# The first matrix of expert n+1 ahead of the second matrix of expert n, in a decoder step with 32 experts

## The chip, the cores and the metric

One core of a Trainium2 chip runs the whole program. The metric is the device time of one execution in microseconds, as the median of several runs of the same program. The engines named below are TensorE (PE in the profile, PEld for its weight loads), VectorE (DVE), ScalarE (ACT), GpSimd (POOL) and SyncE (SP). SP does nothing but wait and issue transfers here.

## The reference, cut to what matters

One layer is applied to 256 prompt tokens and 8 sample tokens that share all weights: a mixer (pooling and a matrix memory), a layer norm, 32 experts of which each token uses four, a second layer norm and a gated embedding. Everything is float32. The part that the change touches is the experts:

```
def run_block(args):
    e, toks, g = args
    xb = xf[toks]
    h = xb @ w1[e] + b1[e]                       # 1024 -> 2048
    glu = jnp.minimum(h[:, ::2], SWIGLU_LIMIT)
    lin = jnp.clip(h[:, 1::2], -SWIGLU_LIMIT, SWIGLU_LIMIT)
    a = glu * jax.nn.sigmoid(SWIGLU_ALPHA * glu) * (lin + 1)
    out = a @ w2[e] + b2[e]                      # 1024 -> 1024
    return out * g[:, None].astype(out.dtype)
...
x2 = layer_norm(DN_ALPHA * x1 + ff, ln2_g, ln2_b)
y = x2 + jax.nn.sigmoid(x2 @ w_ple_gate) * (p.astype(x2.dtype) @ w_ple)
```

All 32 experts' weights are read once from HBM: 8 MiB of `w_mlp1` and 4 MiB of `w_mlp2` for each.

## The kernel before

**The weight ring.** `ring` has 16 slots of 1 MiB (8 KiB in each of 128 partitions). An expert takes 12 units of one slot: 8 for its first matrix, 4 for its second. SP loads them two at a time ("a pair", 2 MiB, `load_pair`, line 396). Units are numbered in order of use, and unit v may be loaded when TensorE has used unit v-16: each use of a unit raises the semaphore `units_used`, and SP waits for it before each pair. So 8 pairs at most are loaded or in flight ahead of TensorE. The first 16 units are loaded during the mixer. Two of them lie in the slots 10 and 11 that hold the state `Cst` until it is written out, so unit 6 waits for the semaphore `C_out` of that store. GpSimd issues that store (line 1900), and after it eight small output transfers (lines 1903 to 1912), the gate table (lines 1914 to 1921) and two loads of layer norm columns (line 1926).

**One expert** (`expert(n, j)`, once each on TensorE, VectorE and ScalarE). A body of `STEP = 4` experts stands in a loop on each engine; `passes` of blocks of 64 places are made, one with these inputs. TensorE's order for expert n is written out by hand:

1. biases of the first matrix (line 870), then 8 units of it (line 883), into `bank[0]` and `bank[1]`. After units 1, 3 and 5 come the three parts of `combine` for expert n-1 (lines 844 and 850): the rows that `eout` holds are spread back to tokens. VectorE adds them to the totals (`accumulate`, lines 1395 and 1400).
2. `gather(n + 1)` (line 822) collects the next expert's rows, `spread_places` (line 836) makes the pattern for the next combine.
3. four transposes of the activation `act_out` (line 907), which VectorE and ScalarE have made in the meantime from `bank[0]` and `bank[1]` (lines 1424 to 1430, sigmoid in line 1744). ScalarE copies the result to `aT` (line 1749).
4. `turn_gathered` (line 857) for the next expert, of which VectorE makes `xgT` (lines 1385 and 1388).
5. bias of the second matrix (line 914), then its 4 units (line 925) into `bank[4]`, which ScalarE copies to `eout` (line 1752).

**Before the loop** stand the routing, `gather(0)`, `turn_gathered`, `spread_places(0)` and the last piece of an early embedding. VectorE starts the totals (line 1460) and ScalarE copies parts of the gate table once GpSimd has made it (lines 1761 and 1765, semaphore `sample_moved`).

**After the loop** TensorE transposes a piece of the embedding's input, waits for `eout`, does the last combine into `LAST_BANKS`, an embedding product (line 975), transposes of the normalised rows (line 988) and the gate product (line 1001). Its weights (`w_ple`, and four loads of `w_ple_gate` into slots 6 to 9, line 464) are issued by SP behind the last expert's.

Of the kernel before, what the change touches and what calls it, by code (L numbers as in the profile page):

```python
# [22 lines left out]
P = 128  # L23
# [13 lines left out]
FF = 1024  # L37
# [13 lines left out]
UNITS = 12  # L51
FIRST = 4
# [45 lines left out]
def build(nc, consts, x_prompt, x_sample, state_pool, state_C, state_n, state_m, p_prompt, p_sample,  # L98
# [4 lines left out]
    with ExitStack() as ctx:  # L103
# [162 lines left out]
        sel = sb("sel", [3 * EXPERTS, 2, P], BF16)  # L266
# [48 lines left out]
        def slot_of(body_unit):  # L315
            return (FIRST + body_unit) % SLOTS

        def landings(body_unit):

            s = slot_of(body_unit)  # L320
            return sum(slot_of(v) == s for v in range(body_unit + 1))
# [6 lines left out]
        def _(sp):  # L328
# [65 lines left out]
            def load_pair(e, j, u):  # L394
                s = slot_of(UNITS * j + u)
                sp.dma_start(pair_place(s), pair_weights(e, u)).then_inc(sem(f"slot{s}"), 16)


            def load_next(n):

                load_pair(n // UNITS, n // UNITS, n % UNITS)

# [15 lines left out]
            load_next(10)  # L418
            sp.wait_ge(sem("hT_ps"), 2)
# [9 lines left out]
            for n in range(SLOTS, UNITS * STEP, 2):  # L429
                sp.wait_ge(sem("units_used"), n - SLOTS + 2)  # L430
                load_next(n)

            def load_body(e, done):

                for n in range(0, UNITS * STEP, 2):
                    sp.wait_ge(sem("units_used"), done + (n - SLOTS + 2))
                    load_pair(e + n // UNITS, n // UNITS, n % UNITS)

            bodies = EXPERTS // STEP
            with sp.Fori(1, bodies) as i:  # L440
                load_body(i * STEP, i * (STEP * UNITS))
            sp.wait_ge(sem("passes_ready"), 1)
            npass = sp.value_load(extra[0:1, 0:1], min_val=0, max_val=PASSES - 1) + 1
            with sp.If(npass > 1):
                with sp.Fori(1, npass) as b:
                    with sp.Fori(0, bodies) as i:
                        load_body(i * STEP, b * (EXPERTS * UNITS) + i * (STEP * UNITS))
            sp.nop()


            used = npass * (EXPERTS * UNITS)

            def wait_slot(s):
                sp.wait_ge(sem("units_used"), used + ((s - FIRST) % SLOTS + 1 - SLOTS))
# [6 lines left out]
            for i in range(4):  # L461
                if 6 + i == 8:
                    wait_slot(9)
                sp.dma_start(ring[:, 6 + i, :].rearrange("p (k n) -> p k n", k=2),
                             w_ple_gate[0, 256 * i:256 * i + 256, :].rearrange("(k p) n -> p k n", p=P))\
                  .then_inc(sem(f"pgate_in{i}"), 16)
# [18 lines left out]
        def _(pe):  # L485
# [374 lines left out]
            def expert(n, j):  # L860

                i4 = n - j

                pe.wait_ge(sem("xgT_done"), n + 1)

                pe.wait_ge(sem("h_read"), n * 2 + 1)
                for t in range(2):
                    for q in range(2):
                        col = FF * t + 512 * q
                        pe.matmul(bank[q][BLOCK * t:BLOCK * (t + 1), :], sel[:, j % 2, 0:BLOCK],  # L870
                                  bias_parts[:, col:col + 512], start=True, stop=False)
                for k in range(KD):
                    u = UNITS * j + k
                    s = slot_of(u)

                    if k % 2 == 0:
                        pe.wait_ge(sem(f"slot{s}"), i4 * 12 + 16 * (before[s] + landings(u)))
                    if k == 5:
# [9 lines left out]

                    if k == 1:
                        pe.wait_ge(sem("out_done"), n + 1)  # L890
                        pe.wait_ge(sem("comb_read"), n * 3 + 1)
                        combine(0, (j + 1) % 2)
                    elif k == 3:
                        pe.wait_ge(sem("comb_read"), n * 3 + 2)
                        combine(1, (j + 1) % 2)
                    elif k == 5:
                        combine(2, (j + 1) % 2)

                pe.wait_ge(sem("onehot_ready"), n * 2 + 4)
                gather(n + 1)  # L900
                pe.wait_ge(sem("hotT_done"), n + 1)
                spread_places((j + 1) % 2)

                for m in range(4):
                    if m == 0:
                        pe.wait_ge(sem("act_ready"), n * 2 + 2)
                    last = pe.transpose(bank[3][:, m * P:(m + 1) * P], act_out[:, m * P:(m + 1) * P], ident)  # L907
                last.then_inc(sem("aT_ps"), 1)
                pe.wait_ge(sem("xg_copied"), n + 2)
                turn_gathered()  # L910

                pe.wait_ge(sem("comb_read"), n * 3 + 4)
                for h in range(2):
                    pe.matmul(bank[4][BLOCK * h:BLOCK * (h + 1), :], sel[:, j % 2, 0:BLOCK],  # L914
                              bias_parts[:, 2 * FF + 512 * h:2 * FF + 512 * h + 512], start=True, stop=False)
                pe.wait_ge(sem("aT_done"), n + 1)
                for k in range(8):
                    u = UNITS * j + 8 + k // 2
                    s = slot_of(u)
                    if k % 4 == 0:  # L920
                        pe.wait_ge(sem(f"slot{s}"), i4 * 12 + 16 * (before[s] + landings(u)))
                    w = ring[:, s, :].rearrange("p (a f) -> p a f", a=2)
# [4 lines left out]
                    if k % 2 == 1:  # L927
                        last.then_inc(sem("units_used"), 1)

# [20 lines left out]
            pe.wait_ge(sem("h_read"), npass * (2 * EXPERTS) + 1)  # L950
            pe.wait_ge(sem("xgT_done"), npass * EXPERTS + 1)
# [6 lines left out]
            pe.wait_ge(sem("hotT_done"), npass * EXPERTS + 1)  # L958
            combine(0, (STEP - 1) % 2, LAST_BANKS[0])
            combine(2, (STEP - 1) % 2, LAST_BANKS[2])  # L960
            pe.wait_ge(sem("xg_copied"), npass * EXPERTS + 1)
# [6 lines left out]
            def gate_weights(k):  # L968
                return ring[:, 6 + k // 2, :].rearrange("p (k n) -> p k n", k=2)[:, k % 2, :]
# [61 lines left out]
        def _(dve):  # L1031
# [372 lines left out]
            def expert(n, j):  # L1404

                for c in range(2):
                    dve.wait_ge(sem("comb_ps"), n * 3 + 1 + c)
                    accumulate(c, n, (bank[7], bank[4]))

                dve.wait_ge(sem("gathered"), n + 1)  # L1410
                dve.wait_ge(sem("out_done"), n + 1)
                one_hot(n + 1, (j + 1) % 2)
                dve.wait_ge(sem("comb_ps"), n * 3 + 3)
                if j == 0:
                    dve.wait_ge(sem("sample_moved"), 7)
                accumulate(2, n, (bank[7], bank[4]))

                for q in range(2):
                    if q == 0:
                        dve.wait_ge(sem("first_half"), n + 1)  # L1420
                    else:
                        dve.wait_ge(sem("units_used"), n * UNITS + 8)
# [3 lines left out]
                    dve.wait_ge(sem("halves_ready"), n * 4 + 2 * q + 2)  # L1426
                    STT(lin[:, q, :], lin[:, q, :], 1.0, glu[:, q, :], ALU.add, ALU.mult).then_inc(sem("h_read"), 1)  # L1427
                    dve.wait_ge(sem("h_read"), n * 2 + q + 2)
                    dve.wait_ge(sem("sig_ready"), n * 2 + q + 1)
# [3 lines left out]
                hot_turned(n + 1, (j + 1) % 2)  # L1433
                turned(n + 1)
# [34 lines left out]
            hot_turned(0, 0)  # L1469
            dve.wait_ge(sem("ple_ps"), 3)  # L1470
# [7 lines left out]
            with dve.Fori(0, npass * EXPERTS, STEP) as n:  # L1478
                for j in range(STEP):
                    expert(n + j, j)  # L1480
# [469 lines left out]
```

## Time and profile before

| | us |
|---|---|
| time, median of 3 runs (lowest, highest) | 1123.28 (1123.21, 1123.94) |
| span of the profiled execution, first to last instruction | 1122.0 |
| the profiled execution's own time, by its span | 1122.0, which is 1.3 below the median of the runs |
| TensorE busy | 1102.2 (98% of the span) |
| VectorE, ScalarE, GpSimd busy | 410.8, 165.4, 78.3 |
| HBM read | 436.61 MB |

The span is that of one execution and leaves out what lies before the first and after the last instruction; times of runs are therefore a little above it. TensorE is called busy while a matmul is in its pipeline, so a high share doesn't say by itself that it sets the time. The DMA share in a stretch is the mean over the core's 16 DMA engines. It can come out a little above 1.00, since a packet is counted where it starts.

### The profile page before, as it was taken

How to read it: one execution, taken by the hardware profiler on the slowest of the kernel's cores; microseconds unless marked ns; L12 is line 12 of the kernel's file. 1: busy time of each engine (PE TensorE's matmuls, PEld its weight loads, DVE VectorE, ACT ScalarE, POOL GpSimd, SP SyncE). 2: the span in 40 equal slices, each digit the busy share in tenths (PEclk: the TensorE clock that was granted, in tenths of full speed). 3: DMA queues.
4: the chain of work that ended last, by engine and by line, in shares of the span. 5: the costliest groups of instructions: out<-in, count | busy, mean ns of one | idle time of the engine just before them, and what ended most of it. 6: DMA issues, size and time to landing. Idle time of an engine off the chain costs nothing.

```text
span 1122.0 us, 14800 instructions
## 1 busy us (share of the span) xinstructions
PE 1102.2 (98%) x5706; PEld 428.6 (38%) x5706; DVE 410.8 (37%) x875; ACT 165.4 (15%) x310; POOL 78.3 (7%) x102
## 2 busy tenths in 40 slices
PE   8999999999999999999999999999999999999998
PEld 6788433333333333333333333333333333323344
DVE  1657583333333333333333333333333333222255
ACT  1423141001000100010001100010001000100033
POOL 0756610000000000000000000000000000000000
PEclk9999999999999999999999999999999999999999
DMA  9986779999999999999999999999999999999961
GB/s 318 261 341 240 253 286 403 427 428 428 429 428 429 429 427 429 427 429 428 430 428 428 429 427 429 429 429 428 428 429 428 429 429 429 427 429 427 428 280 39
DMA packets 47699, 440.45 MB, mean 393 GB/s; under 512 B 10512, under 2 KB 11788, under 8 KB 22741
## 3 DMA queue, kind: packets, MB, share of 16 engines
q1 hardware_dynamic: 46489, 436.94, 93.8%
q0 software_dynamic: 896, 2.66, 0.8%
q10 hardware_dynamic: 292, 0.56, 0.1%
q8 instruction: 13, 0.21, 0.1%
q14 instruction: 9, 0.07, 0.0%
HBM read 436.61 MB, written 3.77 MB: 392 GB/s over the span
## 4 chain that ended last, share of the span: by engine, by line
PE 87%; DMA 10%; DVE 2%; ACT 0%; issue 0%; SPq 0%; DVEq 0%; ACTq 0%
PE bank L883 36%; PE bank L925 18%; DMA ring<-in_w_mlp 9%; PE bank L822 7%; PE bank L510 6%; PE bank L844 5%; PE bank L1001 2%; PE bank L686 2%; PE bank L857 2%; PE bank L907 2%; PE bank L870 1%; PE bank L914 1%; PE bank L850 1%; DMA ring<-in_w_in 1%; PE bank L836 1%
## 5 line engine op out<-in xcount | busy, mean ns | idle before, releaser
L883 PE MATMUL bank<-ring,proj 128*64 128x512 f32 x2048 | 466.0, 597 | 4.7 <-DMA ring<-in_w_mlp 4.7
L1395 DVE SCALAR_TENSOR_TENSOR xT<-bank,proj,xT 128x512 f32<-128x512 f32 x128 | 90.2, 747 | 440.9 <-PE bank L844 439.5
L883 PEld LDWEIGHTS bank<-ring,proj 128*64 128x64 f32 x2048 | 135.3, 136 | 288.7 <-issue 246.9
L925 PE MATMUL bank<-ring,wpool 128*64 128x512 f32 x1024 | 225.1, 592 | 0.0
L925 PEld LDWEIGHTS bank<-ring,wpool 128*64 128x64 f32 x1024 | 71.2, 136 | 130.0 <-issue 129.2
L1744 ACT ACTIVATE proj<-proj 128x256 f32<-128x256 f32 x64 | 26.7, 417 | 546.7 <-DVE proj L1424 546.7
L822 PE MATMUL bank<-xreg,proj 128*64 128x512 f32 (+1 forms) x396 | 95.4, 599 | 0.1
L510 PE MATMUL bank<-xT,ring 128*128 128x264 f32 x320 | 76.3, 396 | 2.9 <-DVE proj L1058 2.4
L844 PE MATMUL bank<-mixT 64*128 64x512 f32 x264 | 74.5, 641 | 0.5 <-ACT mixT L1752 0.5
L510 PEld LDWEIGHTS bank<-xT,ring 128*128 128x128 f32 x320 | 61.4, 195 | 15.6 <-DVE proj L1058 2.8
L1752 ACT COPY mixT<-bank 128x512 f32<-128x512 f32 x32 | 18.8, 586 | 232.4 <-PE bank L925 232.4
L1424 DVE TENSOR_SCALAR proj<-bank 128x256 f32<-128x256 f32 x64 | 26.7, 417 | 67.4 <-PE bank L883 67.4
L822 PEld LDWEIGHTS bank<-xreg,proj 128*64 128x64 f32 (+1 forms) x396 | 25.3, 134 | 64.7 <-issue 64.7
L1400 DVE SCALAR_TENSOR_TENSOR hist_mix<-bank,proj,hist_mix 128x128 f32<-128x128 f32 x66 | 20.1, 347 | 70.1 <-PE bank L850 70.1
L1430 DVE TENSOR_TENSOR proj<-proj 128x256 f32<-128x256 f32 x64 | 38.8, 605 | 5.0
L844 PEld LDWEIGHTS bank<-mixT 64*128 64x128 f32 x264 | 19.9, 184 | 52.9 <-issue 52.9
L1385 DVE TENSOR_TENSOR proj<-bank,ln_rows_of_pairs 128x512 f32<-128x512 f32 x33 | 22.8, 692 | 19.2 <-PE bank L857 19.1
L686 PE MATMUL bank<-ring,mixT 128*128 128x512 f32 x64 | 28.7, 597 | 0.1
L1001 PE MATMUL bank<-ring 128*128 128x512 f32 (+1 forms) x80 | 28.2, 509 | 0.2 <-issue 0.2
L1427 DVE SCALAR_TENSOR_TENSOR proj<-proj 128x256 f32<-128x256 f32 x64 | 27.2, 425 | 2.2
L1425 DVE TENSOR_SCALAR proj<-bank 128x256 f32<-128x256 f32 x64 | 26.3, 411 | 0.0
L857 PE MATMUL bank<-cst,hist_mix 128*128 128x128 f32 x132 | 24.6, 309 | 0.2 <-ACT hist_mix L1755 0.2
(339 smaller groups left out, 633.6 us busy)
## 6 DMA issues: line engine op xcount, KB each, us to landing
ring<-in_w_mlp SPq DMA_DIRECT2D x192, 2048.0 KB, 23.8
ring<-in_w_in SPq DMA_DIRECT2D x10, 1024.0 KB, 12.4
ring<-in_w_out SPq DMA_DIRECT2D x4, 1024.0 KB, 8.4
ring<-in_w_ple_gate SPq DMA_DIRECT2D x4, 1024.0 KB, 27.9
xreg<-in_x_prompt SPq DMA_DIRECT2D x4, 512.0 KB, 4.7
ring<-q_row SPq DMA_DIRECT2D x1, 2048.0 KB, 7.1
ring<-k_row SPq DMA_DIRECT2D x1, 2048.0 KB, 7.0
out<-ring POOLq DMA_DIRECT2D x1, 2048.0 KB, 14.2
```

The lines of the kernel that those rows point to most:

```text
L510: last = pe.matmul(bank[t % 2][:, 0:TOK], w[:, k % 4, j * P:(j + 1) * P], xT[:, k, :], start=(k == 0), stop=(k == KD - 1))
L686: last = pe.matmul(banks[half][0:n, :], mixT[:, k, t0:t0 + n], w[:, k % 2, half * 512:half * 512 + 512], start=(k == 0), stop=(k == KD - 1))
L822: last = pe.matmul(bank[2][BLOCK * h:BLOCK * (h + 1), :], onehot[0:m, c, 0:BLOCK], xtok[0:m, c, 512 * h:512 * h + 512], start=(c == 0), st ...
L844: last = pe.matmul(banks[h][:, :], hotT[half, buffer, c * P:(c + 1) * P], eout[half, :], start=True, stop=True)
L857: last = pe.transpose(bank[6][:, q * P:(q + 1) * P], xg_of_pairs[:, q // 2, q % 2, :], ident)
L883: last = pe.matmul(bank[q][BLOCK * t:BLOCK * (t + 1), :], xgT[:, k % 4, k // 4, :], ring[:, s, col:col + 512], start=False, stop=(k == KD ...
L925: last = pe.matmul(bank[4][BLOCK * h:BLOCK * (h + 1), :], aT[:, m, BLOCK * t:BLOCK * (t + 1)], w[:, k % 2, 512 * h:512 * h + 512], start=F ...
L1001: last = pe.matmul(GATE_BANKS[c][i], x2T[:, k, t0:t0 + n], gate_weights(k)[:, PIECES[c][i]], start=(k == 0), stop=(k == KD - 1))
L1395: ins = STT(total[:, c, s], ins_bank[h][:, :], gate_table[:, c, bass.ds(n, 1)], total[:, c, s], ALU.mult, ALU.add)
L1424: TS(glu[:, q, :], hb[:, 0, :], LIMIT, None, ALU.min).then_inc(sem("halves_ready"), 1)
L1427: STT(lin[:, q, :], lin[:, q, :], 1.0, glu[:, q, :], ALU.add, ALU.mult).then_inc(sem("h_read"), 1)
L1430: TT(act_out.rearrange("p (a q x) -> p q x a", a=4, q=2)[:, q], lin[:, q, :].rearrange("p (x a) -> p x a", a=4), sig[:, q, :].rearrange("p ...
```

## The change

TensorE's order becomes, for step n: the first matrix of expert n+1 with the combine of expert n-1 in it, `gather(n + 2)`, `spread_places`, the first half of the second matrix of expert n, `turn_gathered`, its second half, and the transposes of the activation of n+1. VectorE and ScalarE follow the same order. The first matrix of expert 0, its activation and `gather(1)` move ahead of the loop, with no combine in them. The loop covers all but the last four experts, whose steps are written out behind it: the last but one step has nothing to gather any more, and the last has no first matrix and does its combine into other banks (`LATE_BANKS`) before the second matrix.

The order of the loads follows the order of use: 8 units of expert 0's first matrix, then in turn 8 units of the first matrix of n+1 and 4 of the second of n. Behind the first matrix of expert 31 eight units are left out, so that the last second matrix lands in the slots 8 to 11, which that first matrix used; the gate's weights go to the slots 1, 3, 6 and 7. `sel` gets four buffers in place of two. The store of `Cst` moves from GpSimd's queue to SP's, behind the load of unit 10, and GpSimd's descriptor scratch is 2048 bytes in place of 8192.

```diff
+LEAD = 8
-        sel = sb("sel", [3 * EXPERTS, 2, P], BF16)
+        sel = sb("sel", [3 * EXPERTS, STEP, P], BF16)
+        GATE_SLOTS = (1, 3, 6, 7)
+        LATE_BANKS = {0: (bank[7], bank[2]), 1: (bank[0], bank[1]), 2: (bank[5], bank[6])}
...
+            def load_next(v):
+                n, u = divmod(v - LEAD, UNITS)
+                if v < LEAD:
+                    load_pair(0, v, v)
+                else:
+                    load_pair(n + 1 if u < 8 else n, v, u)
...
             sp.wait_ge(sem("Cnew_done"), 1)
             load_next(10)
+            sp.dma_start(C_sample[0].rearrange("b h v k -> v (b h) k"), Cst).then_inc(sem("C_out"), 16)
...
+            def load_body(e, done, following):
+                for r in range(0, UNITS * STEP, 2):
+                    j, u = divmod(r, UNITS)
+                    first = u < 8
+                    if first and j == STEP - 1 and following is None:
+                        continue
+                    sp.wait_ge(sem("units_used"), done + (LEAD + r - SLOTS + 2))
...
+            tail = npass * (EXPERTS * UNITS) - STEP * UNITS
+            load_body(last, tail, None)
...
+            def step(n, j, ahead=2):
+                i4 = n - j
+                v0 = LEAD + UNITS * j
+                if ahead >= 1:
+                    first_matrix(n + 1, j + 1, v0, i4, n)
+                    if ahead == 2:
+                        pe.wait_ge(sem("onehot_ready"), n * 2 + 6)
+                        gather(n + 2)
+                    pe.wait_ge(sem("hotT_done"), n + 1)
+                    spread_places((j + 1) % STEP)
+                    pe.wait_ge(sem("comb_read"), n * 3 + 4)
+                else:
+                    pe.wait_ge(sem("h_read"), n * 2 + 3)
+                    pe.wait_ge(sem("hotT_done"), n + 1)
+                    pe.wait_ge(sem("xg_copied"), n + 1)
+                    pe.wait_ge(sem("out_done"), n + 1)
+                    pe.wait_ge(sem("comb_read"), n * 3 + 1)
+                    for c in range(3):
+                        combine(c, (j + 1) % 2, LATE_BANKS[c])
+                second_matrix(n, j, v0 + 8, i4, range(0, 4))
+                if ahead == 2:
+                    pe.wait_ge(sem("xg_copied"), n + 3)
+                    turn_gathered()
+                second_matrix(n, j, v0 + 8, i4, range(4, 8))
+                if ahead >= 1:
+                    turn_activation(n + 1)
...
+            first_matrix(0, 0, 0, 0)
+            pe.wait_ge(sem("onehot_ready"), 4)
+            gather(1)
+            turn_activation(0)
+            pe.wait_ge(sem("xg_copied"), 2)
+            turn_gathered()
             pe.wait_ge(sem("ln1_in"), 48)
...
-            with pe.Fori(0, npass * EXPERTS, STEP) as n:
+            with pe.Fori(0, npass * EXPERTS - STEP, STEP) as n:
                 for j in range(STEP):
-                    expert(n + j, j)
+                    step(n + j, j)
+            for j in range(STEP):
+                step(npass * EXPERTS - STEP + j, j, min(2, STEP - 1 - j))
...
(VectorE, ahead of the loop)
+            dve.wait_ge(sem("gathered"), 1)
+            one_hot(1, 1)
...
+            dve.wait_ge(sem("sample_moved"), 7)
+            activate(0, LEAD)
+            turned(1)
...
(ScalarE, in a step)
+                act.wait_ge(sem("units_used"), n * UNITS + (LEAD + UNITS if ahead else LEAD + UNITS - 8))
                 act.copy(eout, bank[4][:, :]).then_inc(sem("out_done"), 1)
+                if ahead >= 1:
+                    turned_activation(n + 1)
...
(GpSimd)
             pool.engine_nop().then_inc(sem("Cnew_done"), 1)
-            pool.dma_start(C_sample[0].rearrange("b h v k -> v (b h) k"), Cst).then_inc(sem("C_out"), 16)
...
-    nc = bacc.Bacc("TRN2", target_bir_lowering=False, num_devices=1, dynamic_dma_scratch_size=8192)
+    nc = bacc.Bacc("TRN2", target_bir_lowering=False, num_devices=1, dynamic_dma_scratch_size=2048)
```

## Rows read from the trace of the kernel before

**Rows 1.** The page: packets of the instruction queue; a small load's size and time to landing.
```profile
q8 instruction: 13, 0.21, 0.1%
...
cst<-in_consts ACTq DMA_DIRECT2D x1, 64.0 KB, 3.9
```
**Rows 2.** Windows: stretch, length, each engine's busy time, clock, DMA share, GB/s.
```profile
160.00:164.00 4.00, 3.75 (x19) 1.33 (x20) 3.76 (x13) 0.59 (x1) 1.32 (x2) 1.00 0.03 12
...
192.00:900.00 708.00, 708.00 (x3659) 232.91 (x3657) 227.45 (x475) 71.94 (x130) 0.00 (x0) 1.00 1.01 428
```
**Rows 3.** Chain that ended last, through one expert: start, length, what.
```profile
502.34 0.43 PE bank L870 x4
502.77 3.44 PE bank L883 x16
506.21 1.06 PE bank L844 x4
...
515.50 0.36 PE bank L850 x16
...
519.44 2.72 PE bank L822 x12
...
522.38 0.59 PE bank L907 x4
...
523.93 6.87 PE bank L925 x32
530.80 0.43 PE bank L870 x4
```
**Rows 4.** Pairs of weights on SP's queue, line 396: when issued, time to landing.
```profile
L396 SPq DMA_DIRECT2D ring<-in_w_mlp x1: 328/328/328, 122.4 to 122.4; - x1
DMA to landing us min/median/max: 8.5/8.5/8.5
...
L396 SPq DMA_DIRECT2D ring<-in_w_mlp x1: 328/328/328, 164.8 to 164.8; - x1
DMA to landing us min/median/max: 9.9/9.9/9.9
...
L396 SPq DMA_DIRECT2D ring<-in_w_mlp x1: 328/328/328, 185.9 to 185.9; - x1
DMA to landing us min/median/max: 8.8/8.8/8.8
...
L396 SPq DMA_DIRECT2D ring<-in_w_mlp x1: 333/333/333, 1036.1 to 1036.1; - x1
DMA to landing us min/median/max: 35.3/35.3/35.3
```
**Rows 5.** Chain that ended last, at the first expert.
```profile
160.67 0.63 PE bank L870 x4
```
**Rows 6.** Timeline at the first expert: start, length, engine, line; [idle before, releaser].
```profile
162.59 3.31 POOL L1921 TENSOR_SCALAR proj<-proj 128x160 f32<-128x160 f32 x3 [24.39 <-DVE proj L1325]
...
167.07 1.69 ACT L1765 COPY hist_mix<-proj 8x256 f32<-8x256 f32 x4
...
180.18 0.60 DVE L1430 TENSOR_TENSOR proj<-proj 128x256 f32<-128x256 f32 x1
...
181.37 0.74 PE L857 MATMUL bank<-cst,hist_mix 128*128 128x128 f32 x4
...
182.87 0.69 DVE L1388 TENSOR_TENSOR proj<-proj,ln_rows_of_pairs 128x512 f32<-128x512 f32 x1
```
**Rows 7.** Chain that ended last, from the last first matrix to the last combine.
```profile
1061.62 3.65 PE bank L883 x16
...
1076.69 0.59 ACT mixT L1752
1077.28 0.23 issue
1077.52 1.13 PE bank L844 x4
```

More of the change, by code:

```diff
@@ L313, in build, with slot_of, landings @@
         PIECES = {0: (slice(0, 512), slice(512, 1024)), 1: (slice(0, 512), slice(512, 768), slice(768, 1024))}
[L315 to L321, printed above, removed]
+        GATE_SLOTS = (1, 3, 6, 7)
+        LATE_BANKS = {0: (bank[7], bank[2]), 1: (bank[0], bank[1]), 2: (bank[5], bank[6])}
+        def slot_of(unit):
+            return (FIRST + unit) % SLOTS
+        def landings(unit):
+            s = slot_of(unit)
+            return sum(slot_of(v) == s for v in range(unit + 1))
         before = [2 if s < 4 else 1 if s < 10 else 0 for s in range(SLOTS)]
@@ L887, in expert @@
                     last.then_inc(sem("units_used"), 1)
+                    if n is None:
+                        continue
                     if k == 1:
@@ L891, in expert, with second_matrix @@
                         pe.wait_ge(sem("comb_read"), n * 3 + 1)
-                        combine(0, (j + 1) % 2)
+                        combine(0, jm % 2)
                     elif k == 3:
                         pe.wait_ge(sem("comb_read"), n * 3 + 2)
-                        combine(1, (j + 1) % 2)
+                        combine(1, jm % 2)
                     elif k == 5:
[L897 to L919, printed above, removed]
+                        combine(2, jm % 2)
+            def second_matrix(n, j, v0, i4, ks):
+                if ks[0] == 0:
+                    for h in range(2):
+                        pe.matmul(bank[4][BLOCK * h:BLOCK * (h + 1), :], sel[:, j, 0:BLOCK],
+                                  bias_parts[:, 2 * FF + 512 * h:2 * FF + 512 * h + 512], start=True, stop=False)
+                    pe.wait_ge(sem("aT_done"), n + 1)
+                for k in ks:
+                    v = v0 + k // 2
                     if k % 4 == 0:
-                        pe.wait_ge(sem(f"slot{s}"), i4 * 12 + 16 * (before[s] + landings(u)))
-                    w = ring[:, s, :].rearrange("p (a f) -> p a f", a=2)
+                        landed(v, i4)
+                    w = ring[:, slot_of(v), :].rearrange("p (a f) -> p a f", a=2)
                     t, m = k // 4, k % 4
@@ L968, in gate_weights @@
             def gate_weights(k):
[L969 removed]
+                return ring[:, GATE_SLOTS[k // 2], :].rearrange("p (k n) -> p k n", k=2)[:, k % 2, :]
             def embedding():
@@ L1402, in accumulate, with activate @@
                 ins.then_inc(sem("comb_read"), 1)
[L1404 to L1416, printed above, removed]
+            def activate(m, used):
                 for q in range(2):
                     if q == 0:
-                        dve.wait_ge(sem("first_half"), n + 1)
+                        dve.wait_ge(sem("first_half"), m + 1)
                     else:
-                        dve.wait_ge(sem("units_used"), n * UNITS + 8)
+                        dve.wait_ge(sem("units_used"), used)
                     hb = bank[q][:, :].rearrange("p (f two) -> p two f", two=2)
@@ L1477, in _ @@
             dve.wait_ge(sem("gates_table"), 1)
-            with dve.Fori(0, npass * EXPERTS, STEP) as n:
+            with dve.Fori(0, npass * EXPERTS - STEP, STEP) as n:
                 for j in range(STEP):
-                    expert(n + j, j)
+                    step_of(n + j, j)
+            for j in range(STEP):
+                step_of(npass * EXPERTS - STEP + j, j, min(2, STEP - 1 - j))
             done = npass * (3 * EXPERTS)
```

116 lines of the change are left out of this document (73 added, 43 removed).

## The prediction

> **What bounds the kernel now.** I read the windows first, then the chain that ended last, then the landing times of the weight pairs. The windows show TensorE busy for all 708 us between 192 and 900, and the DMA engines too, at 428 GB/s [rows 2]. One of the two only looks like the bound. A pair is 2 MiB, which at 428 GB/s is 4.90 us, so an expert's six pairs take 29.4 us. TensorE takes 530.80 - 502.34 = 28.46 us for an expert [rows 3]. The transfers are slower by 0.94 us an expert, and the 16 slots only hide that for a time. Near the end TensorE waits for the weights. The landings say the same: the pair issued at 164.8 lands at 174.7, the last one at 1036.1 + 35.3 = 1071.4, with 183 pairs in between: 4.90 us each, without a pause [rows 4]. TensorE alone would need 160.67 + 32 x 28.46 = 1071.4 to end the experts [rows 3, 5]; it ends them at 1076.69, where `eout` is copied [rows 7]. So three things set the time: when the stream of pairs starts for good, whether it is ever interrupted, and what follows its last pairs.
>
> The stream has one real pause. From 160 to 164 the DMA share is 0.03 [rows 2]: the slots are full, and the next pair is issued at 164.8, when TensorE has used the first two units (160.67 + 0.63 for the biases + about 3.44) [rows 3 to 5]. There is a small second one. The fifth pair after the pause would land at 174.7 + 4 x 4.90 = 194.3; it is issued only at 185.9 and lands at 194.7 [rows 4]. That is 0.4 us lost.
>
> **The change in the steady state: nothing.** The order is there to take the activation and its transposes out of TensorE's way, but they stand in no one's way: in the chain through an expert TensorE goes from line 822 over 836 to the four transposes (0.59 us) without a gap, since the gather of 2.72 us covers VectorE and ScalarE [rows 3]. Every matmul of an expert stays, so TensorE's period stays 28.46 us. I looked for new waits. The combine needs `eout` of n-1, copied while the biases and two units run (0.43 + 3.44 against 0.59 for the copy). `turn_gathered` comes 3.4 us behind the gather. `xgT` has the second half, 3.4 us, and the transposes for its 2.2 us (from the start of line 857 to the end of 1388 [rows 6]). All are covered. Without cover they would be paid only beyond 0.94 us an expert, as the transfers hide that much.
>
> **Ahead of the loop.** The wait before the first matmul is the same (`xgT` of expert 0), so the first release stays at 164.8. `one_hot(1, 1)` is inserted behind what that wait needs. Without combines the next three releases come 1.1, 2.1 and 2.5 us earlier, which only lengthens the queue. TensorE ends the matrix at 160.67 + 0.63 + 4 x 3.44 = 175.1, the gather at 177.8. Before, the matrix of expert 0 ended at 178.0 (the same sum with its combines and units of 3.58) and its activation at 180.78 [rows 6], 2.8 us later. Now the activation ends at 177.9, the transposes at 178.5. The copy of the gathered rows also ends about 178.5, `turn_gathered` starts at 178.6 and `xgT` is ready 2.2 us later, at 180.8: an exposed stall of 1.5 us, once. TensorE starts expert 1 at 180.9 and frees the fifth pair at 180.9 + 0.63 + 3.43 = 185.0. To land at 194.3 it must be issued 8.5 us before, the landing time of a pair in a quiet queue [rows 4], that is by 185.8. So the 0.4 us is won, with 0.8 us of margin. Later releases, from the same rows, are at 189.6, 194.3, 198.2 and, behind a gather, 204.9; the places in the stream ask for 190.7, 195.6, 200.5 and 205.4. The last margin, 0.5 us, is the smallest.
>
> A rule bears on this. The Trainium skill, page "DMA: Bandwidth & Descriptors", section "Anatomy of one DMA", gives a transfer about 2.0 us plus its bytes over 436 GB/s, 6.8 us for a pair as an estimate by that page. Then the old issue at 185.9 would have been early enough and there would be no 0.4 us to win: a gain of 0.85 us in place of 1.25. The trace's 8.5 us disagrees with it.
>
> **The other moved transfers.** The store of the state goes to SP's queue, between the pair of unit 10 and the layer norm row, the early `w_ple`, and unit 6, which waits for it on either queue. The bytes are the same. It is paid in the time before 160.6, and behind it lies the pause: 4 us and more could be added to those transfers before the stream starts later. Unit 6 is first used at 160.67 + 0.63 + 3 x 3.44 = 171.6. I take nothing. Without the pause as cover it would cost its delay in full.
>
> **The end.** Count the stream from its end, 1071.4 - 0.4 = 1071.0. The last pairs are now: first matrix of 31 complete at 1051.4, second matrix of 30 at 1056.3 and 1061.2, of 31 at 1066.1 and 1071.0. The last two may be issued only when units 6 and 7 of that first matrix, and the two before them, are used, about 1055.1 and 1050.3. At 1055.1 the queue still has over 6 us of work, and 1071.0 - 1055.1 = 15.9 us is well over 8.5, so there is no pause. The gate's weights stay behind them. TensorE: second half of 30 from 1061.2, 3.5 us, ends 1064.7. The copy to `eout` 0.6 and the wait 0.2 as at 1077.28 [rows 7], 1065.5 (the transposes, 0.59, run beside it). Three combines 1.13 + 1.06 + 0.36, biases 0.34, 1068.4. Then 6.87 [rows 3] for the second matrix, whose last pair is needed at 1071.9 and is there: 1075.3. It is 1076.6 before, so 1.3 us is gained. The bound is the combine, which depends on the pair of 1061.2 and so keeps the 0.4. What follows (copy, combine, embedding, gate) is the same, and moves up.
>
> **The sum.** 0 for 31 steps, -0.4 in the stream, -0.85 at the end: -1.25 us. The profiled execution, 1122.0, becomes 1120.75; the runs' median lies 1.3 above the span, so 1122.0.
>
> **Rivals.**
>
> *A part of the program arrives late (slower).* Four steps stand outside the loop and must be loaded as TensorE comes to them; the instruction queue moved only 13 packets of 16 KB in the whole execution [rows 1]. TensorE's 708 of 708 busy us [rows 2] speak against any price of jumping back, but that code is resident. A late part costs TensorE the time of a small load, at most the 3.9 us of 64 KB [rows 1]. In the first three steps the wait for weights swallows it. In the last step, after 1061.2, it is paid: -1.25 + 3.9 = +2.65, 1125.9. It decides from 3.5 us, that is 0.2% and what is gained.
> The Trainium skill, page "Runtime: NRT & Kernel Launch", section "Instruction fetch mechanics", says that straight code is fetched ahead and mostly hidden, while a taken branch out of the two resident pages stalls. By that rule it is the loop that would have paid; the trace shows it paid nothing, and so the rule takes none of this rival's chance.
>
> *The smaller scratch holds GpSimd up (slower).* Were its eight small stores to wait for each other, some 8.5 us each, 60 us, the gate table would be late. It has 24.4 us of idle before line 1921, and ScalarE's copies end at 168.8, some 5 us before expert 0's activation needs them [rows 6]. The next 30 us would be paid one to one, since the fifth pair is freed behind that activation: 1153. The largest store has left that queue, which speaks against it.
>
> *Expert 0's activation is late (slower).* It is the same place at a smaller size: past 185.8 each us costs one us. A forecast of slower needs 4.3 us more than I count, about 1125.
>
> *The first pair lands as in a quiet queue (faster).* It takes 9.9 us at 164.8, against 8.5 [rows 4]. GpSimd's column loads fall beside it. If these come elsewhere, 1.4 us more is won, 1120.6, which is 0.24% below. They should be only 0.6 us later, so this is not likely, but it also stands for a larger gain at the end than I count.
>
> *The reordering does nothing at all.* The stream ends at 1071.4 and the end gains 0.85: 1122.4, still within 0.2%.
>
> **How the numbers follow.** Forecast with the last rival, 0.60; faster, 0.20; late code, 0.13; scratch, 0.03; late activation, 0.04. Two parts in a thousand, 2.2 us, is about what a measurement of this kernel can tell from no change. So: faster 0.20, same 0.60, slower 0.20. The forecast's own range is 1121.1 to 1122.9. For 8 in 10 it reaches down past the quiet landing to 1119.8 and up to the late code, 1125.9.
>
> **What would show it.** Right: no gap in TensorE's chain through an expert and a period of 28.46 up to about 900; a fifth pair landing 19.6 us behind the first; the last pair about 1071.0; second matrix of 31 ended near 1075.3. Wrong: a stall of TensorE behind the gather beyond 1.5 us before expert 1, a DMA share under 0.9 anywhere between 170 and 1070, a gap without weights or engine as its cause behind the loop, or a last pair off by over 1 us.

## The result, and the profile after

| | median of the runs | lowest to highest | profiled execution |
|---|---|---|---|
| before | 1124.1 us (14 runs) | 1123.21 to 1125.31 | 1122.0 span |
| changed | 1127.08 us (14 runs) | 1125.55 to 1130.46 | 1130.31, span 1128.5 |

The ratio is 1.0033, 95% interval 1.0022 to 1.0043: slower, where 1122.0 and no measurable difference were forecast, and outside the range. The runs of the changed kernel don't lie around one value. Five lie between 1125.55 and 1126.02, with a granted clock of 1.0, three near 1127, one is at 1128.68, and five lie at 1130.3 to 1130.5, with a clock of 0.995 to 0.997. So there are two things to explain: 2.3 us between the lowest runs (1125.55 - 1123.21), and what makes 1126 into 1130.

The chain that ended last, through one expert, as [rows 3]. In the changed kernel the first matrix is line 907, the second 939, the gathered rows' transposes 879, the activation's 948, the biases 895 and 929, the gather 844:

```profile
502.21 3.44 PE bank L907 x16
...
518.87 2.72 PE bank L844 x12
...
522.14 3.44 PE bank L939 x16
525.58 0.67 PE bank L879 x4
526.25 3.58 PE bank L939 x16
529.84 0.59 PE bank L948 x4
530.42 0.56 PE bank L895 x4
530.98 3.44 PE bank L907 x16
```

From matrix to matrix it is 530.98 - 502.21 = 28.77 us, not 28.46. Set it beside [rows 3]. The second matrix took 6.87 in one piece; here it takes 3.44 + 3.58. The biases behind it took 0.43; here, behind the transposes of line 948, they take 0.56. The gathered rows' transposes take 0.67 for 0.63. That is 0.15 + 0.13 + 0.04 = 0.32, in instructions that nobody added. Two rows of the kernel before belong to this reading, a unit behind a combine and the gathered rows' transposes:

```profile
507.27 3.58 PE bank L883 x16
...
522.96 0.63 PE bank L857 x4
```

The windows, as [rows 2]: the changed kernel at the start of expert 1 and in the last stretch of the loop, and under them that last stretch in the kernel before:

```profile
184.00:192.00 8.00, 8.00 (x32) 2.32 (x30) 1.41 (x2) 0.00 (x0) 0.00 (x0) 0.80 0.98 381
900.00:1071.00 171.00, 171.00 (x877) 54.56 (x877) 54.00 (x112) 14.93 (x29) 0.00 (x0) 1.00 1.01 427
```
```profile
900.00:1071.00 171.00, 166.26 (x862) 54.54 (x860) 54.59 (x114) 16.84 (x31) 0.00 (x0) 1.00 1.01 428
```

From 192 to 900 TensorE is busy for 708 of 708 us, as before, which says nothing. The row of 900 to 1071 tells which one is the bound: TensorE had 4.7 us of idle there, now it has none. The landings and the profile's page say it from the other side (a pair on SP's queue, as [rows 4]; the instruction queue; the first matrix's row in the changed kernel and, as L883, in the kernel before, where the number behind the last bar is its idle time):

```profile
L401 SPq DMA_DIRECT2D ring<-in_w_mlp x1: 328/328/328, 1036.8 to 1036.8; - x1
DMA to landing us min/median/max: 30.0/30.0/30.0
```
```profile
q8 instruction: 17, 0.28, 0.1%
...
L907 PE MATMUL bank<-ring,proj 128*64 128x512 f32 x2048 | 467.2, 598 | 0.0
```
```profile
L883 PE MATMUL bank<-ring,proj 128*64 128x512 f32 x2048 | 466.0, 597 | 4.7 <-DMA ring<-in_w_mlp 4.7
```

The second pair of expert 30's second matrix lands at 1036.8 + 30.0 = 1066.8, 2.8 us before TensorE comes to it (1066.11 + 3.44). Before, TensorE waited for pairs there. Expert 1's start and the end of the chain, as [rows 5] and [rows 7]:

```profile
183.25 0.13 issue
183.38 0.66 PE bank L895 x4
184.03 5.10 PE bank L907 x16
```
```profile
1066.11 6.90 PE bank L939 x32
...
1073.85 1.99 PE bank L866 x8
...
1076.54 6.89 PE bank L939 x32
...
1083.45 0.59 ACT mixT L1831
```

Sixteen matmuls of line 907 take 5.10 us where their like take 3.44, and the granted clock of 184 to 192 is 0.80: the lower level, 1.2 GHz, for 3.4 us, right behind TensorE's idle of 1.6 us. Expert 0 had started at 163.27 for 160.67, 2.6 us late. Two things are in that. The 32 matmuls of line 532 from 10.4 us on took 10.41 us, where their like in the kernel before (line 510) took 9.44; and the 32 from 47.4 on, where the granted clock was 0.87, took 9.02 for 7.39. The copy behind the last second matrix starts at 1083.45 for 1076.69. Of these 6.8 us, 2.6 are the late start, 1.7 the clock at 184, and 2.5 are left for the schedule. So the profiled run is one of the upper group, and 2.6 + 1.7 = 4.3 us is what lies between 1126.0 and 1130.3.

### The profile page after: what moved, and what is told of

It reads as the page before. It is cut to its first block, busy times and chain, and to the rows that moved or that the text cites. A ratio compares the mean times of both kernels' runs of the same rounds, so it can differ in the third digit from the quotient of the medians.

```text
span 1128.5 us, 14658 instructions
## 1 busy us (share of the span) xinstructions
PE 1111.7 (99%) x5689; PEld 423.9 (38%) x5689; DVE 407.8 (36%) x870; ACT 155.7 (14%) x302; POOL 74.0 (7%) x101
## 4 chain that ended last, share of the span: by engine, by line
PE 96%; DVE 2%; DMA 1%; ACT 0%; issue 0%; SPq 0%; DVEq 0%; ACTq 0%
PE bank L907 40%; PE bank L939 20%; PE bank L844 7%; PE bank L532 6%; PE bank L866 6%; PE bank L1055 2%; PE bank L708 2%; PE bank L879 2%; PE bank L948 2%; PE bank L895 2%; PE bank L872 1%; PE bank L929 1%; DMA ring<-in_w_in 1%; PE bank L858 1%; PE bank L1075 0%
## 5 line engine op out<-in xcount | busy, mean ns | idle before, releaser
L939 PE MATMUL bank<-ring,wpool 128*64 128x512 f32 x1024 | 231.7, 595 | 0.0
L844 PE MATMUL bank<-xreg,proj 128*64 128x512 f32 (+1 forms) x384 | 92.5, 599 | 0.1
L532 PE MATMUL bank<-xT,ring 128*128 128x264 f32 x320 | 78.9, 406 | 2.8 <-DVE proj L1112 2.4
L879 PEld LDWEIGHTS bank<-cst,hist_mix 128*128 128x128 f32 x128 | 17.7, 207 | 24.8 <-issue 24.3
```

Source lines behind the costliest of these rows:

```text
L532: last = pe.matmul(bank[t % 2][:, 0:TOK], w[:, k % 4, j * P:(j + 1) * P], xT[:, k, :], start=(k == 0), stop=(k == KD - 1))
L844: last = pe.matmul(bank[2][BLOCK * h:BLOCK * (h + 1), :], onehot[0:m, c, 0:BLOCK], xtok[0:m, c, 512 * h:512 * h + 512], start=(c == 0), st ...
L879: last = pe.transpose(bank[6][:, q * P:(q + 1) * P], xg_of_pairs[:, q // 2, q % 2, :], ident)
L939: last = pe.matmul(bank[4][BLOCK * h:BLOCK * (h + 1), :], aT[:, m, BLOCK * t:BLOCK * (t + 1)], w[:, k % 2, 512 * h:512 * h + 512], start=F ...
```

## The experiments

Theory A: each change of TensorE between 64-column matmuls and full-width transposes costs it some 0.14 us; the changed kernel makes one more such trip (to transposes and back) an expert, and so TensorE has become the bound. Rivals: a wait (C), or something else in the new order. Theory B, for the other part: the clock fell at 184 us because TensorE had been idle for 1.6 us.

**e1: one trip, grouped.** Both groups of transposes stand behind the placing of rows, the second matrix is whole.

```diff
                     spread_places((j + 1) % STEP)
+                    pe.wait_ge(sem("aT_done"), n + 1)
+                    turn_activation(n + 1)
+                    if ahead == 2:
+                        pe.wait_ge(sem("xg_copied"), n + 3)
+                        turn_gathered()
...
-                second_matrix(n, j, v0 + 8, i4, range(0, 4))
-                if ahead == 2:
-                    pe.wait_ge(sem("xg_copied"), n + 3)
-                    turn_gathered()
-                second_matrix(n, j, v0 + 8, i4, range(4, 8))
-                if ahead >= 1:
-                    turn_activation(n + 1)
+                second_matrix(n, j, v0 + 8, i4, range(0, 8))
```

> The changed kernel with its two groups of transposes put back between spread_places and the biases of the second matrix, side by side, and the second matrix in one piece; the new order of experts stays. Theory A (TensorE pays about 0.14 us each time it goes from the 64-column matmuls of a matrix to transposes and back, and the change made two such trips out of one): the period of a step falls from 28.77 to 28.45 us, TensorE has slack again, and the weights set the end. Sum: 1124.1 - 1.25 + up to 1.7 for a clock drop before expert 1 = 1122.9 to 1124.5. Rival B (the new order itself or its waits in the middle of the second matrix cost the 0.32 us): the period stays above 28.6 us and the time near 1126.

Its chain:

```profile
514.88 0.65 PE bank L948 x4
515.53 0.56 PE bank L879 x4
...
516.43 6.87 PE bank L939 x32
523.30 0.43 PE bank L895 x4
...
1018.96 35.12 DMA ring<-in_w_mlp
...
1060.69 0.66 PE bank L948 x4
```

The period is 540.40 - 511.94 = 28.46 and the weights are in the chain again. The time was not better: 1129.52, ratio 1.0041 (1.0026 to 1.0056), at clocks of 0.992 to 0.998; the profiled run was 1125.88. Two things are in it. In the last step but one no gather covers VectorE and ScalarE, so TensorE waits there from 1056.96 to 1060.69 for the activation of expert 31. That is worth 1.0 us: the profiled run of e8, which differs in this step alone, takes 1124.88 and ends its last second matrix at 1078.0 for 1079.0, with the last pair landed at the same time in both (1073.7 and 1073.6). The rest of the median is the lower clock of e1's runs, lower than in the other kernels here, which no run explains. So the period confirms A, and the time, 1122.9 to 1124.5 by the expectation, doesn't.

**e2: one more trip in the kernel before.** `turn_gathered` goes between the halves of its second matrix; nothing else changes.

```diff
-                pe.wait_ge(sem("xg_copied"), n + 2)
-                turn_gathered()
...
                 for k in range(8):
+                    if k == 4:
+                        pe.wait_ge(sem("xg_copied"), n + 2)
+                        turn_gathered()
```

> The kernel before, with one thing of the change: turn_gathered stands between the two halves of the second matrix. Theory A: the period goes from 28.46 to 28.65 us (second half 3.58 for 3.44, the transposes 0.68 for 0.63), TensorE alone then needs 32 x 28.65 = 916.8 us from 160.67, so it ends the experts at about 1077.5, and the time is 1 us above before. Rival B (the order of experts costs it): the period stays 28.46 us and the time that of before.

```profile
503.36 0.60 PE bank L907 x4
...
503.99 0.59 ACT wpool L1749
...
504.70 3.65 PE bank L925 x16
508.35 0.68 PE bank L857 x4
509.03 3.58 PE bank L925 x16
```

1144.51, ratio 1.0173 (1.0157 to 1.019), period 529.71 - 500.43 = 29.28. It is 19 us more than before, where 1 was expected: `turn_gathered` had also covered ScalarE's copy of the turned activation, which now stands in the chain. It shows both kinds of cost (3.58 behind the transposes, in the old kernel too), but mixed with a wait.

**e3: the wait alone.** The kernel before, with a wait in the middle of the second matrix that is already satisfied, and nothing moved.

```diff
+                    if k == 4:
+                        pe.wait_ge(sem("xg_copied"), n + 2)
```

> The kernel before, with only a wait between the two halves of the second matrix, on a semaphore that has long been reached; no work is moved. Theory A: the period stays 28.46 us. Rival C (a wait, or the register arithmetic for it, in the middle of the matrix breaks the stream of matmuls): the second half takes 3.58 us instead of 3.44.

1124.49 in one run; the second matrix is 6.87 in one piece, the period 28.46. Rival C is out, in the order of the kernel before.

**e4: one trip, side by side.** The changed kernel with both groups in the middle of the second matrix.

```diff
-                second_matrix(n, j, v0 + 8, i4, range(4, 8))
                 if ahead >= 1:
                     turn_activation(n + 1)
+                second_matrix(n, j, v0 + 8, i4, range(4, 8))
```

> The changed kernel with both groups of transposes side by side in the middle of the second matrix. Theory A: the trip at the end of the step is gone, the biases behind the matrix take 0.43 for 0.56 us and the second group of transposes about as before: the period is 28.6 us, halfway, and the time about halfway between the changed kernel and the grouped one, 1124 to 1125.5. Rival B: 28.77 us, no change.

```profile
514.83 3.44 PE bank L939 x16
518.27 0.67 PE bank L879 x4
518.94 0.44 PE bank L948 x4
519.38 3.58 PE bank L939 x16
522.96 0.43 PE bank L895 x4
...
1026.64 35.43 DMA ring<-in_w_mlp
...
1062.11 3.68 PE bank L939 x16
...
1069.31 6.90 PE bank L939 x32
```

The second group costs 0.44 where it stands beside the first, for 0.59 by itself, and the biases 0.43 for 0.56: the trip that is gone shows at both its ends. The period is 540.06 - 511.56 = 28.50, a little under the 28.6 expected, and the weights are the bound. Against the kernel before the halved matrix still costs its 0.15 (3.44 + 3.58 for 6.87), but the eight transposes are 0.11 cheaper (0.67 + 0.44 for 0.59 + 0.63), and in e1, side by side in the other order, they are not (0.65 + 0.56). So the price of a group goes by its neighbours, but not by the number of trips alone, and no run shows why this order is the cheaper one. The time is 1125.62, ratio 1.0006 (0.9994 to 1.0017); at clock 1.0 it is 1123.1; on the same chip the kernel before is at 1123.26 to 1124.19 with a clock of 0.999 or more. The changed kernel's loss is gone by moving one group of four transposes past half a matrix. The copy behind the last second matrix starts at 1076.23 for 1076.69.

**e9: one trip more.** The changed kernel with its gathered rows turned two and two.

```diff
-                second_matrix(n, j, v0 + 8, i4, range(0, 4))
+                second_matrix(n, j, v0 + 8, i4, range(0, 2))
                 if ahead == 2:
                     pe.wait_ge(sem("xg_copied"), n + 3)
-                    turn_gathered()
+                    turn_gathered((0, 1))
+                second_matrix(n, j, v0 + 8, i4, range(2, 4))
+                if ahead == 2:
+                    turn_gathered((2, 3))
```

> The changed kernel with its four transposes of gathered rows split into two and two, behind a quarter and behind a half of the second matrix: the same instructions, one more change from matrix to transposes and back. Theory A (each change of kind costs TensorE about 0.14 us on the way back and some 0.05 to 0.1 on the way in): period 28.95 to 29.0 us, and since TensorE is the bound about 30 times as much at the end, 1131 to 1133 us at clock 1.0. Rival (what lengthened the period is that the gathered rows' transposes now lie beside the weights' arrival, or something else that does not go by the number of changes): period 28.77, 1125.6 to 1126.

```profile
525.97 1.72 PE bank L940 x8
527.68 0.44 PE bank L879 x2
528.12 1.87 PE bank L940 x8
529.99 0.43 PE bank L879 x2
530.42 3.58 PE bank L940 x16
```

The period is 535.15 - 506.03 = 29.12. The trip costs 0.35: 0.15 on the way back (1.87 for 1.72) and 0.20 on the way in (0.87 for 0.67). I had counted only half of the second. The run took 1140.75; the changed kernel's profiled run, in which expert 0 began at the same time and the clock fell at the same place, 1130.31. That is 10.4 more, and 30 x 0.35 is 10.5; the 1131 to 1133 of the expectation were for a run without a fall of the clock (4.3 us less) and had too small a price for the trip. It is one run. TensorE is the bound, and pays the trip in full.

**e0: the changed kernel again,** on the chip of e5, e7 and e8.

> The changed kernel itself, beside the others on one chip. Theory A (TensorE is the bound at 28.77 us an expert, because its half-matrix and transpose groups now alternate once more): 1125.5 to 1126 us where the granted clock is 1.0 throughout, about 1.7 us more for each stretch of 3.41 us at the lower clock, so a ratio near 1.002 to 1.004 again and a period of 28.77 us in the profile. Rival (the chip or the moment made it slow): a period of 28.46 us and a time near 1123.

1128.6, ratio 1.0025 (1.0013 to 1.0037). Four of ten runs at 1125.74 to 1126.04, one at 1127.12, five at 1130.08 to 1130.31. The profile repeats the first one.

**e5: work in the stall.** Four f32 matmuls of 128 x 512 into a bank nobody reads, before expert 1.

```diff
             turn_gathered()
+            pe.wait_ge(sem("ple_done"), 3)
+            for _ in range(4):
+                pe.matmul(bank[7][:, :], ident, cst[:, 0:512], start=True, stop=True)
```

> The changed kernel, with four extra full-width f32 matmuls into an unused bank in the 1.6 us stall before expert 1's first matrix; their result is not read. Theory B (the stall is what the clock fell behind at 184 us): the first group of 16 matmuls of expert 1 takes 3.44 us in place of 5.10, the profile's span is about 1.7 us shorter than the changed kernel's and the runs gather at the fast end, 1125.6. Rival (the fall of the clock has nothing to do with the stall and comes as chance has it): the spread of the runs, 1125.5 to 1130.5, and the share of runs below clock 1.0 stay as they were. Either way the period stays 28.77.

The profile has no fall near 184 us (3.43 for line 907), but it can't decide: its expert 0 began at 161.74, and e1, which began at 161.56 and has no filler, has no fall there either. And the filler was too long: 3.44 us in a stall of 1.6, and TensorE is the bound, so it pays the rest. 1130.07, ratio 1.0044 (1.0031 to 1.0057), five runs from 1128.69 to 1130.7. The time can't decide either; e10 is the same with half the filler.

**e10: work that fits.** Two of these matmuls, not four.

> The changed kernel with two extra f32 matmuls in the stall before expert 1 (1.72 us by the last run's rows, where the stall is 1.60, so that TensorE is busy through it and expert 1 starts 0.2 us later at most). Theory B (TensorE's idle 1.6 us is what the lower clock at 184 us followed): no run at 1130.3, the latest ones near 1128.6, the earliest at 1125.8, and a ratio of 1.001 to 1.003. Rival: the two groups of runs, near 1125.8 and near 1130.3, stay.

```profile
178.80 1.72 PE bank L998 x4
180.52 0.56 PE bank L895 x4
181.08 3.44 PE bank L907 x16
```

1127.16, ratio 1.002 (1.001 to 1.003). Four runs at 1125.72 to 1126.05, two at 1127.1 to 1127.2, four at 1128.53 to 1129.19. The kernel without filler had 10 of its 24 runs at 1130.08 to 1130.46 and one at 1128.68. The upper group has moved down by the 1.7 us of one fall of the clock and the lower one is where it was, as theory B has it. That is shown by the times of ten runs; the profile above is of a run of the lower group, whose expert 0 began at 160.29, and no profile here shows an upper run with filler. The fall without filler occurs on e10's chip too (e9).

**e8: grouped, but for the last step.** e1, with the activation's transposes behind the second matrix in the last step but one.

> The changed kernel with both groups of transposes between line 866's placing of rows and the biases, so that the second matrix runs whole, but in the last step that still has a first matrix ahead of it the transposes stay behind the second matrix, as in the changed kernel. Theory A: period 28.46 as in the kernel before, the weights bound again from about 1000 us on, the second matrix of expert 31 ends near 1076.0 (0.5 to 0.7 earlier than before) and the time at clock 1.0 is 1122.6 to 1123.2, no more than 0.1% under the kernel before. Rival (the loss of the grouped run lies not in its last steps but in the grouping itself): 1125.8 as there.

Its ninth pair behind the pause, on SP's queue:

```profile
L401 SPq DMA_DIRECT2D ring<-in_w_mlp x1: 328/328/328, 206.2 to 206.2; - x1
DMA to landing us min/median/max: 9.5/9.5/9.5
```

1125.0, ratio 1.0008 (0.9997 to 1.0019); at clock 1.0 1123.77 to 1125.12, more than I expected. Period 28.46, but both groups now stand ahead of the pair that frees the ninth slot: it is issued at 206.2, in e4 at 204.8, and lands at 215.7 for 214.2. The stream never makes that up (the last half of expert 30 starts at 1063.90, in e4 at 1062.11). So 1.5 of these 1.8 us are the price of one release that is late by 0.8 by the prediction's own count (205.4). e1 has the same order there.

**e7 and e11: the best of both.** e4 with four, and with two, filler matmuls.

> Both groups of transposes side by side in the middle of the second matrix, and four extra f32 matmuls in the stall before expert 1. Theory A and B together: period 28.50, no fall of the clock near 181 us, 1122.6 to 1123.1 at clock 1.0, a ratio of 0.999 to 1.000 against the kernel before. Rival to B: the same share of runs with the clock below 1.0 as without the extra matmuls (median 1125.6 there, 1123.1 to 1128.2).

1125.85, ratio 1.0013 (1.0004 to 1.0023). The long filler frees the fifth pair at 186.6, 0.8 behind the 185.8 that the prediction asks for; it lands at 195.6 for 194.2, the ninth pair at 216.6 for 214.2, and the last second matrix ends at 1078.64 for 1076.21. The expectation left that out, and missed.

> Both groups of transposes side by side in the middle of the second matrix, with two extra f32 matmuls in the stall. The stream of weights is the bound again, and its fifth pair is freed at about 185.2 to 185.4, near enough to the 184.9 of the kernel without them: the second matrix of expert 31 ends within 0.5 us of 1076.2, 1123.1 to 1123.5 at clock 1.0, ratio 0.999 to 1.001. Rival to B: runs of 1127.6 and over are as frequent as without the extra matmuls.

1124.18, with the kernel before at 1125.54 beside it: 0.9992 (0.9982 to 1.0002). The last second matrix ends at 1076.69, its lowest run is 1122.77, the kernel before's 1123.29. Its highest run is 1126.24, where e4 has five of ten from 1126.61 to 1128.16, which again speaks for theory B, with the two on different chips. It has the lowest ratio here, and is not told apart from the kernel before, nor from e4.

**b0: the kernel before again.**

> The kernel before itself. If the lower clock near the start of the execution is the chip's and not the change's, a profile of it may show expert 0 starting at 160.7, 161.8 or 163.3 us, and the time goes with it: about 1123.3, 1124.6 or 1126.5; the period is 28.46 in any case.

Its window of 40 to 50 us, and the changed kernel's:

```profile
40.00:50.00 10.00, 10.00 (x40) 7.17 (x39) 3.99 (x14) 4.59 (x7) 8.67 (x18) 0.84 1.07 304
```
```profile
40.00:50.00 10.00, 8.95 (x35) 6.38 (x36) 5.09 (x16) 5.58 (x9) 8.66 (x18) 0.87 1.08 302
```

1124.7, with expert 0 at 161.85. The early fall of the clock is in the kernel before too.

## Why the prediction was wrong

**What bounded the kernel before: right.** e1, e4, e8 and e11 have the weights in the chain again as soon as the period is 28.5.

**The step that failed: "Every matmul of an expert stays, so TensorE's period stays 28.46 us."** Counting instructions missed that the price of a group depends on the group ahead of it. The row was there: the first units' matmuls take 3.44 behind the biases [rows 3] and 3.58 behind a combine (507.27, shown with the result), and the prediction itself used "units of 3.58". The change gives each expert one more place of that kind. The term was put at 0; it is 0.31 to 0.32 an expert, some 9.5 us of TensorE over 30 steps.

**The step that should have caught it: "paid only beyond 0.94 us an expert".** It is wrong too. 0.94 is what the transfers are slower per expert, but TensorE starts with all 16 slots full and far ahead, and the two meet only near the end. What counts is the room left there. TensorE's work from expert 0 to the last second matrix is 1078.86 - 160.29 = 918.6 us in e10, the changed order in a run where the clock never fell and no weight is waited for. With 0.31 less in each of 30 steps it would be 909.3. The stream allows 915.6 (e4, 1076.23 - 160.66). That is 6.3 us of room, 0.21 an expert: the 0.04 of e4 disappears in it, 0.31 overflows it, and the 0.35 more of e9 is paid whole. Against the kernel before, with 916.0 for the same stretch, the changed one is 2.6 longer, where its lowest run is 2.3 longer. The prediction had the numbers for the old order: 1076.69 - 1071.4, 0.17 an expert.

**Ahead of the loop: right, but for what the stall does.** In e4 the fifth pair is released at 184.9 (predicted 185.0), the next at 189.5, 194.2, 198.1 and 204.8 (189.6, 194.3, 198.2, 204.9), and the fifth lands at 194.2 (194.3). The stall is 1.6 us (1.5). Its price was counted as time alone. In the changed kernel the clock fell behind it in two profiles of two; that costs 1.7 us, paid in full because TensorE is the bound. With a filler that fits, the times lose it (e10).

**The end: right in mechanism, too large.** 1.3 us was forecast; e4, which has the order without the extra trip, gains 0.5. The fifth pair's 0.4 was won and lost again: the last pair lands at 1071.8 for 1071.4, forecast 1071.0. The second half of expert 30 starts at 1062.1, not 1061.2, and that is the difference. The tenth pair behind the pause still lands 0.3 ahead of the kernel before's (219.1 for 219.4), the last one 0.4 behind; where in between the 0.7 went, no run shows. The prediction's own margins for the next four pairs were 1.1, 1.3, 2.3 and 0.5 us.

**What was taken at nothing.** The store of the state on SP's queue cost nothing: expert 0 starts at 160.66 in e4. The smaller scratch: GpSimd's idle ahead of the gate table is unchanged at 24.4 us. Late code: 17 packets of instructions for 13, and no gap behind the loop, so that rival, which held the upper end of the range, didn't happen. The quiet landing did happen in part (9.3 us for 9.9 in e4) and brought nothing that reached the end.

**The rule on transfers.** Issued at 206.2 behind a queue that was busy until 209.3, e8's ninth pair took 9.5 us and landed 1.5 late. By the 6.8 us that the prediction estimated from the Trainium skill, page "DMA: Bandwidth & Descriptors", section "Anatomy of one DMA", it would have been in time. The pairs disagree with that estimate here as well; but that section measured its figure on transfers issued by GpSimd, and the pairs are issued by SP, so the prediction carried it to a queue that the section doesn't speak of.

**None of the rivals was this one.** Each slower case was a wait or a late arrival; that TensorE's own work could grow with no instruction added was given no chance.

## What to carry to other kernels

Cost a reordering by neighbours, not by instructions: read from the rows what a group takes behind each kind of group, and count how often the kind changes; here one more trip to transposes and back in a step of 28.46 us turned a transfer-bound kernel into a TensorE-bound one. The room for an engine beside a slower stream is the distance at the end of the loop over the number of steps, not the difference of the two rates. And where an engine becomes the bound, everything that the transfers hid (a fall of the clock, a stall once) is paid from then on.

## What the runs showed of the hardware

**A change of form costs TensorE.** A group of 16 matmuls of 64 columns takes 3.44 us behind its own kind (the biases have 64 columns too) and 3.58 behind 128-wide transposes or a combine; 8 take 1.72 and 1.87. The activation's four transposes take 0.59 behind a matrix and 0.44 behind the gathered rows' four (e4); the gathered rows' four take 0.67 behind a matrix, and behind the activation's 0.63 in the kernel before and 0.56 in e1. So a neighbour of the same form makes a group cheaper by 0.04 to 0.15, and the rows don't say what sets the size. The weight loads show where the change is paid (the timeline of the changed kernel):

```profile
524.55 0.14 PEld L939 LDWEIGHTS bank<-ring,wpool 128*64 128x64 f32 x2 [0.29 <-issue]
525.51 0.55 PEld L879 LDWEIGHTS bank<-cst,hist_mix 128*128 128x128 f32 x4 [0.81 <-issue]
526.18 0.20 PEld L939 LDWEIGHTS bank<-ring,wpool 128*64 128x64 f32 x4
```

Inside the matrix loads come every 0.43 us and hide under matmuls. The first load for the transposes starts at 525.51, 0.07 before the matrix ends, after 0.81 of idle, and the first load of the second half at 526.18, 0.07 before the transposes end (526.25): across a change of form it is hardly hidden. That this load is the whole price is argued from the rows, not shown. The Trainium skill, page "TensorE: Matmul & The Clock Gate", section "The mechanism", says in its list of what overlaps that a weight load overlaps matmuls in flight only where its row group differs; further up the same section also lets a load be pulled ahead into a background weight buffer. Here loads with all 128 rows hide under matmuls with all 128 rows as long as the column halves alternate, so the trace doesn't agree with the sentence in the list; it doesn't speak against the other one.

**The clock falls for about 3.4 us at a time, and its place matters.** At 184 us the granted clock is 0.80 over 8 us and 0.99 over the 8 before them: 1.7 us of clock lost, which at half the clock are 3.4 us. Eight of the 14 profiles of this study have one such fall between 30 and 60 us, one of the kernel before (b0) among them. Without it expert 0 starts at 160.29 to 160.85 (six profiles), with it at 161.56 to 161.86 (five) or at 163.26 to 163.28 (three, whose matmuls from 10.4 us on had also taken 1.0 us longer). All 14 have an idle of TensorE of 2.4 us that ends near 40 us. In b0, e1, e2 and e3 the fall is in the matmuls right behind it (5.35 to 5.52 us for 3.83); in the changed kernel, e0, e5 and e9 it comes 6.3 us later, with TensorE busy in between (9.01 to 9.05 for 7.39); in six it doesn't come. The second fall, behind the 1.6 us stall, came in all three profiles whose expert 0 began at 163.3 (the changed kernel twice, e9), and in none of e1, e4 and e8, with the same stall and a beginning at 160.7 to 161.6. So an idle goes ahead of these falls but isn't enough for one. What decides stays open.
